# Norms folded into the stages that use them, in two token halves, with x spilled to DRAM tile by tile

## The reference

```python
# block 1
h = _modulate(x, norm_mix_w, sh1, sc1)
x = x + g1 * _merge(...)
x = x + g2 * _swiglu(_modulate(x, norm_ffn_w, sh2, sc2), w_ffn_gate, w_ffn_up, w_ffn_down)
# block 2
h = rms_norm(x) * (1 + sc1) + sh1
u = h @ w_in                      # feeds four mixers: ssd, attention, mlstm, hyena
x = x + g1 * (concatenate([y_ssd, y_na, y_ml, y_hy]) @ w_out)
h = rms_norm(x) * (1 + sc2) + sh2
x = x + g2 * ((silu(h @ ffn_w_gate) * (h @ ffn_w_up)) @ ffn_w_down)
return rms_norm(x, final_norm_g)
```

## Time and profile before

| | |
|---|---|
| median of three runs | 4113.08 us |
| the profiled execution, its own time | 4116.84 us |
| its span, first to last instruction | 4114.8 us |
| PE busy | 3665.1 us, 89% of the span |
| DVE busy | 1719.8 us, 42% |
| ACT busy | 1010.2 us, 25% |
| POOL busy | 106.5 us, 3% |
| mean granted TensorE clock | 0.921 |
| DMA | 279.54 MB, mean 68 GB/s |

### The profile page before, as it was taken

The page is one execution under the profiler, slowest core; times in us unless marked ns, Lnnn a source line. Parts: engine busy times, 40 slices in busy tenths (PEclk is TensorE's granted clock), DMA queues, the critical chain, the costliest instruction groups (busy, mean ns, idle before and its releaser), DMA issues. The chain is left out here.

```text
span 4114.8 us, 40002 instructions
## 1 busy us (share of the span) xinstructions
PE 3665.1 (89%) x15842; PEld 2752.2 (67%) x15842; DVE 1719.8 (42%) x2951; ACT 1010.2 (25%) x1635; POOL 106.5 (3%) x180
## 2 busy tenths in 40 slices
PE   7769999988879997999999797797868779999997
PEld 4345565655668776888888576675446658888885
DVE  4334431435532315444444545335574333334334
ACT  1434422212242213111111323252110131111112
POOL 0000000000010000000000000100000000000000
PEclk8888899899689998999999898898979889999999
DMA  5300020000033212222221213314223111111110
GB/s 206 134 25 1 1 100 31 11 21 11 1 105 120 92 73 92 77 92 82 72 82 61 89 57 78 99 58 138 54 92 138 46 51 41 51 51 51 41 51 41
DMA packets 72797, 279.54 MB, mean 68 GB/s; under 512 B 10424, under 2 KB 29880, under 8 KB 54873
## 3 DMA queue, kind: packets, MB, share of 16 engines
q1 hardware_dynamic: 35080, 166.63, 11.8%
q0 software_dynamic: 20928, 102.66, 6.8%
q10 hardware_dynamic: 16656, 8.42, 1.3%
HBM read 246.11 MB, written 31.59 MB: 67 GB/s over the span
## 5 line engine op out<-in xcount | busy, mean ns | idle before, releaser
L1720 PE MATMUL banks<-input_parts,weight_parts 128*128 128x512 f32 x1408 | 549.9, 391 | 47.1 <-DVE weight_parts L1772 47.1
L1721 PE MATMUL banks<-input_parts,weight_parts 128*128 128x512 f32 x1408 | 549.6, 390 | 0.0
L1722 PE MATMUL banks<-input_parts,weight_parts 128*128 128x512 f32 x1408 | 549.5, 390 | 0.0
L1720 PEld LDWEIGHTS banks<-input_parts,weight_parts 128*128 128x128 f32 x1408 | 265.7, 189 | 103.8 <-issue 48.7
L1785 DVE TENSOR_TENSOR before_split<-before_split,banks 128x512 f32<-128x512 f32 x88 | 60.6, 688 | 594.5 <-PE banks L1722 594.5
L1794 DVE SCALAR_TENSOR_TENSOR x<-banks,parameters,x 128x512 f32<-128x512 f32 x352 | 254.8, 748 | 126.9 <-PE banks L1722 126.6
L1722 PEld LDWEIGHTS banks<-input_parts,weight_parts 128*128 128x128 f32 x1408 | 265.5, 189 | 55.3
L1721 PEld LDWEIGHTS banks<-input_parts,weight_parts 128*128 128x128 f32 x1408 | 265.5, 189 | 55.2
L1720 PE MATMUL banks<-hidden_parts,weight_parts 128*128 128x512 f32 x704 | 273.9, 389 | 0.0
L1721 PE MATMUL banks<-hidden_parts,weight_parts 128*128 128x512 f32 x704 | 273.9, 389 | 0.0
L1722 PE MATMUL banks<-hidden_parts,weight_parts 128*128 128x512 f32 x704 | 273.9, 389 | 0.0
(11 more groups left out here) (496 smaller groups left out, 5971.4 us busy)
## 6 DMA issues: line engine op xcount, KB each, us to landing
weight_ring<-in_w_gu SPq DMA_DIRECT2D x44, 1024.0 KB, 4.8
weight_ring<-in_mod_w POOLq DMA_DIRECT2D x24, 1024.0 KB, 5.3
weight_ring<-in_w_down SPq DMA_DIRECT2D x22, 1024.0 KB, 4.8
weight_ring<-in_w_merge SPq DMA_DIRECT2D x24, 512.0 KB, 3.6
weight_ring<-in_dft SPq DMA_DIRECT2D x12, 1024.0 KB, 5.0
x<-in_x_t POOLq DMA_DIRECT2D x2, 4096.0 KB, 18.0
weight_ring<-in_w_ada_rest POOLq DMA_DIRECT2D x8, 1024.0 KB, 5.4
work<-in_w_ada_rest POOLq DMA_DIRECT2D x8, 1024.0 KB, 5.3
```

Of the source, the lines that this page charges most:

```text
L1720: e.matmul(bank, w_hi, hi, start=(k == 0), stop=False)
L1721: e.matmul(bank, w_hi, lo, start=False, stop=False)
L1722: mm = e.matmul(bank, w_lo, hi, start=False, stop=(k == len(terms) - 1))
```

## The change

The squares of x are made where x is written: in `linear_split` and in the last step of `ffn`, ScalarE squares each piece after its eviction and VectorE adds the squares up over the tiles (`Squares`). `SplitNorm` takes the place of the stages norm_ffn_1, norm_ffn_2, scales_2 and norm_mix_2. It runs at the start of `ffn` and of the stage "projections": one ones-matmul per half, both Ln ahead of both Exp, then scale and parts of the first token half, the first weights, and scale and parts of the second half. TensorE starts on the first half when that is ready, and waits for the second half ahead of bank q = 2 (in `ffn`) or piece 1 (in the projections). x goes to DRAM in 8 DMAs of 512 KB, each after its tile's last eviction, on SyncE. norm_final uses the ready sums, and the output is stored in four DMAs of 1 MB from the scaled pieces. `norm` (norm_mix and norm_final) makes all Ln ahead of all Exp. In ssd_outputs all 10 tokens and in mlstm's outputs all 8 come ahead of the outputs on TensorE, and ScalarE makes the second chunk's exponentials in ssd ahead of the first tokens. A group whose slot was held by single-tile weights is split one piece later. `alternate` goes to another place and is loaded at the start of the projections.

```diff
+class Squares:
+    def __init__(self, pg):
+        m = Mem(pg.big, M_H, M_PARTS)
+        self.sums, self.buf = m(2, HALF), m(2, HALF)
+        self.x = pg.x
+        self.squared, self.added = pg.shared_sem("norm_squares", 2 * KT), pg.shared_sem("norm_added", 2 * KT - 2)
+    def square(self, e, i):
+        tile, s = divmod(i, 2)
+        if i >= 4:
+            self.added.wait(e, i - 3)
+        dst = self.sums[:, s, :] if i < 2 else self.buf[:, s, :]
+        e.activation(dst, self.x[:, tile, s * HALF:(s + 1) * HALF], ACT.Square).then_inc(self.squared.sem, 1)
+    def add(self, e, i):
+        s = i % 2
+        self.squared.wait(e, i + 1)
+        if i >= 4:
+            self.added.wait(e, i - 3)
+        e.tensor_tensor(self.sums[:, s, :], self.sums[:, s, :], self.buf[:, s, :], ALU.add).then_inc(self.added.sem, 1)
...
+class SplitNorm:
+    def __init__(self, pg, scale, shift, high, low, y, rs=None, kept=None):
+        self.pg, self.scale, self.shift, self.high, self.low, self.y, self.kept = pg, scale, shift, high, low, y, kept
+        self.squares = pg.squares
+        self.rs = pg.squares.sums if rs is None else rs
+        self.ms, self.rt = pg.shared_sem("norm_sums", 2), pg.shared_sem("norm_roots", 2)
+        self.scaled, self.rounded, self.split = (pg.shared_sem(f"norm_{n}", 2 * KT) for n in ("scaled", "high", "split"))
+    def half(self, s):
+        return slice(s * HALF, (s + 1) * HALF)
+    def sums(self, e):
+        for s in range(2):
+            e.matmul(self.pg.ps[:, s, :], self.pg.ones, self.squares.sums[:, s, :], start=True, stop=True).then_inc(self.ms.sem, 1)
+    def roots(self, e):
+        rs = self.rs
+        for s in range(2):
+            self.ms.wait(e, s + 1)
+            last = e.activation(rs[:, s, :], self.pg.ps[:, s, :], ACT.Ln, bias=self.pg.eps[:, 0:1], scale=1.0 / D)
+        self.pg.achain(e)(last)
+        for s in range(2):
+            e.activation(rs[:, s, :], rs[:, s, :], ACT.Exp, scale=-0.5).then_inc(self.rt.sem, 1)
+    def take_high(self, e, s):
+        for k in range(KT):
+            self.scaled.wait(e, KT * s + k + 1)
+            e.activation(self.high[:, k, self.half(s)], self.y[:, k, self.half(s)], ACT.Identity,
+                         bias=self.shift(k)).then_inc(self.rounded.sem, 1)
+    def take_low(self, e, s):
+        if self.kept is not None and s == 0:
+            e.wait_ge(self.kept, 16 * KT)
+        self.rt.wait(e, s + 1)
+        h = self.half(s)
+        for k in range(KT):
+            e.scalar_tensor_tensor(out=self.y[:, k, h], in0=self.pg.x[:, k, h], scalar=self.scale(k), in1=self.rs[:, s, :],
+                                   op0=ALU.mult, op1=ALU.mult).then_inc(self.scaled.sem, 1)
+        for k in range(KT):
+            self.rounded.wait(e, KT * s + k + 1)
+            e.scalar_tensor_tensor(out=self.low[:, k, h], in0=self.y[:, k, h], scalar=self.shift(k),
+                                   in1=self.high[:, k, h].bitcast(F32), op0=ALU.add, op1=ALU.subtract).then_inc(self.split.sem, 1)
...
             tiles(4, KT)
-        for g in range(1, NG):
-            weights(g)
+        weights(1)
+        for g in range(NG):
+            if g + 2 < NG:
+                weights(g + 2)
+            for q in range(fills):
+                i = fills * g + q
+                e.wait_ge(pg.ps_free, f0 + i + 1)
+                squares.square(e, i)
...
+                if fills * g + q >= 4:
+                    squares.add(e, fills * g + q - 2)
...
+        for i in range(NG * fills - 2, NG * fills):
+            squares.add(e, i)
...
-        for s, w in enumerate(spans):
+        for s, w in enumerate(spans if squares is None else []):
             for k in range(KT):
                 e.activation(dst(s)[:, k, :], src(s)[:, k, :], ACT.Square).then_inc(sq.sem, 1)
         for s, w in enumerate(spans):
             ms.wait(e, s + 1)
-            ch(e.activation(rs[:, s, 0:w], pg.ps[:, s, 0:w], ACT.Ln, bias=pg.eps[:, 0:1], scale=1.0 / D))
+            last = e.activation(rs[:, s, 0:w], pg.ps[:, s, 0:w], ACT.Ln, bias=pg.eps[:, 0:1], scale=1.0 / D)
+        ch(last)
+        for s, w in enumerate(spans):
             e.activation(rs[:, s, 0:w], rs[:, s, 0:w], ACT.Exp, scale=-0.5).then_inc(rt.sem, 1)
         if shift is not None:
             for s, w in enumerate(spans):
                 for k in range(KT):
...
+            if squares is not None:
+                e.matmul(pg.ps[:, s, :], pg.ones, squares.sums[:, s, :], start=True, stop=True).then_inc(ms.sem, 1)
+                continue
...
+        for k in range(KT if spill else 0):
+            e.wait_ge(pg.ps_free, first_fill[NS - 1] + 2 * k + 2)
+            e.dma_start(spill[0][:, k, :], x[:, k, :]).then_inc(spill[1], 16)
...
+                if n == 0 and q % 2 == 0:
+                    norm.split.wait(e, KT * (q // 2 + 1))
...
+        norm.sums(e)
...
+            elif n == NS - 1:
+                hid_split.wait(e, 2 * FT)
+                for q in range(16):
+                    e.wait_ge(pg.ps_free, first_fill[n] + q + 1)
+                    squares.square(e, q)
+        norm.roots(e)
+        norm.take_high(e, 0)
         take_high(0, 0)
+        norm.take_high(e, 1)
...
+                    if n == NS - 1 and q >= 4:
+                        squares.add(e, q - 2)
+                if n == NS - 1:
+                    squares.add(e, 14)
+                    squares.add(e, 15)
             modulate(mods(n)[1], i)
+        norm.take_low(e, 0)
         take_low(0, 0)
+        norm.take_low(e, 1)
         if mod:
             row_ready.wait(e, 1)
...
-                at = max(at, self.last[same[-1]] + (self.first[g] - self.last[same[-1]] > 1))
+                old = same[-1]
+                at = max(at, self.last[old] + (self.freed[old] is None or self.first[g] - self.last[old] > 1))
...
+            if p < 2:
+                self.norm.split.wait(e, KT * (p + 1))
...
-            yield 4
+            yield SSD_PACE
             s2_rd.wait(e, c + 1)
             for hh in range(4):
                 mm = e.matmul(pg.ps[:, 2 + c % 2, hh * 64:hh * 64 + 64], Mm[:, c % 2, hh, :], XB[:, c, hh * 64:hh * 64 + 64],
                               start=True, stop=True)
             mm.then_inc(y_rd.sem, 1)
-            yield SSD_PACE - 4
     def scalar(e):
...
-            yield SSD_PACE
+            if c:
+                yield SSD_PACE
+        yield SSD_PACE
...
-            yield 3
+            yield ML_PACE
             if c:
                 y_cp.wait(e, c)
             for hh in range(4):
...
-            yield ML_PACE - 3
...
-        self.proj.landed(e, "hy")
-        e.dma_start(self.alt, pg.d["alternate"]).then_inc(self.tables.sem, 16)
...
-        self.tables.wait(e, 48)
+        self.tables.wait(e, 32)
...
+    norm_2 = SplitNorm(pg, lambda k: pg.sc2a[:, k:k + 1], lambda k: pg.mod2[:, k:k + 1], pg.mix_high, pg.mix_low, x,
+                       Mem(pg.big, M_STAGED, M_END)(2, HALF), pg.kept)
...
+    pg.alt = pg.pp[:, 0:P + 1]
...
+        e.wait_ge(pg.stage_done, 3 * after)
+        e.dma_start(pg.alt, pg.d["alternate"]).then_inc(proj.tables.sem, 16)
...
+    def tensor(e):
+        norm_2.sums(e)
+        whole(first["tensor"])(e)
+    def scalar(e):
+        norm_2.roots(e)
+        norm_2.take_high(e, 0)
+        proj.highs(e, 0)
+        norm_2.take_high(e, 1)
+        whole(first["scalar"])(e)
+    def vector(e):
+        e.tensor_scalar(pg.sc2b, pg.mod2[:, 32:40], 1.0, None, ALU.add)
+        pg.vchain(e)(e.tensor_scalar(pg.sc2a, pg.mod2[:, 8:16], 1.0, None, ALU.add))
+        norm_2.take_low(e, 0)
+        proj.lows(e, 0)
+        norm_2.take_low(e, 1)
+        whole(first["vector"])(e)
+    pg.stage(name="projections", sync=sync, gpsimd=pool, tensor=tensor, scalar=scalar, vector=vector)
...
+    def store(e, scaled):
+        for n in range(4):
+            s, k = divmod(4 * n, KT)
+            scaled.wait(e, 4 * (n + 1))
+            at = slice(s * HALF, (s + 1) * HALF)
...
-            e.dma_start(out, result).then_inc(stored, 16)
-            e.wait_ge(stored, 16)
+            e.wait_ge(pg.stored, 64)
```

148 lines of the change are left out of this document (48 added, 100 removed).

## The result

| | before | after |
|---|---|---|
| time, median (us) | 4112.01 (4108.95 to 4113.71, 4 runs) | 4038.93 (4029.26 to 4044.17, 4 runs) |
| ratio, 95% interval | | 0.982 (0.9801 to 0.984) |
| the profiled execution: time, span (us) | 4116.84, 4114.8 | 4044.17, 4042.5 |
| mean granted clock | 0.921 | 0.920 |

The change saves 73 us. I had forecast 4032, with a range of 4018 to 4051; the forecast's own case ran from 4023 to 4041. The time is in both, 7 us above the figure. The kernel before has 4112.01 here, and not the 4113.08 given above, because a fourth run has been added to its three.

The account below looks back on a forecast made before the run. TensorE was taken as busy for 89% of the span, with time lost only where it stands still. The terms summed to -80.9 us, taking the median from 4113.08 to 4032 us, range 4018 to 4051.

Parts of the forecast that it names:

- The start of the FFNs: At ffn_1 and ffn_2, squares and second-half scaling leave TensorE's path: -18.5 us each, bounds -15 to -20.
- ffn_1 to the projections: Ahead of the projections, first matmul 22.4 us earlier, but piece 1 waits 4 to 5: -15 us, bounds -8 to -18.
- The end: At the final norm and store, scaling starts earlier and the last 1 MB store follows: -12.7 us, bounds -8 to -13.5.
- ssd: In ssd's output chunks, six uncovered stalls of 2.1 to 2.2 us replace the old stalls: -1 us, bounds -5 to +7.
- mlstm: In mlstm's output chunks, outputs cover the wait for the mix, but the spread comes late: -12 us, bounds -4 to -19.
- The late split: Behind ssd_out, ScalarE's weights wait no longer holds TensorE at the barrier for 4.72 us: -4 us, bounds -5 to 0.
- (a): Second halves of the split norms late everywhere: 3.5 us at each FFN, 5 at the projections; 4044 us, 12%.
- (b): The woven stages move their stalls and do not remove them: ssd at +7, mlstm at -4; 4048 us, 14%.
- (c): The woven stages gain all, with the clock held: mlstm -19, ssd -5; 4021 us, 9%.
- (d): One table load less at each of four norms, since one set holds Ln and Exp: -5 us, 4027 us, 4%.
- (e): The last part of x's copy to DRAM lands late and the projections' scaling waits 7 us; 4039 us, 5%.
- (f): A 2 us stall at every chunk keeps the clock low through both woven outputs: up to +140, 4172 us; 2%.

Follow-up runs that it names:

- the combined kernel: The kernel after with ssd's outputs behind 6 tokens and ahead of 4, FFNs' first weights on VectorE, early table load, Ln and Exp per half: 4009.47 us.

## Why the prediction was right, and where it was off

**The start of the FFNs (-18.5 each; measured -17.4 and -16.7).** Right in mechanism: no wait came ahead of the third bank, the second half was never late. One overlap was wrong, and with it a term: "4.7 from the barrier to the first scaling, the two ones-matmuls run beside the table load". They do not. The load is issued behind ScalarE's wait for the first sum, so it was 6.74 at ffn_2 and 5.9 at ffn_1. The run with the early load showed that the load alone is not the whole error: the second sum is late as well, and only both edits together give 4.8.

**ffn_1 to the projections (-15; -15.9).** The copy of x held nothing, piece 1 waited 5.64. The late root cost 1.8 us here too (6.51 for 4.7) and piece 1 waited a little longer than forecast; the stretch behind made that good, which lies within the spread of 3 us and is not explained further.

**The end (-12.7; -11.7).** The same late root, 1.2 of it.

**The first norm (+1.5; +1.56).** Right, and shown alone.

**ssd (-1; +1.8 by the means, -0.7 with the order alone on the kernel before, a single profile).** The six bare stalls came exactly as described. Neither figure can be told from nothing in a stretch that the clock spreads over 4 us. I took the clock to be a wash between old and new stalls; that it is worth 5 us once the stalls go was not in my text.

**mlstm (-12; -15.6).** Two terms were too small: the stalls shrank by 12.2 and not 9.4, and the clock gave 6.3 and not 2.6 (with the order alone). I had set the chunk at its length without any low clock and so made the spread late too often.

**The late split (-4; -5.5) and `alternate` (-0.7; -1.3).** The 4.7 us at the barrier go as described, but TensorE's restart, to which I credited the gain, is not what counts: the stretch ends when the attention's values land, and GpSimd, held by the same wait of ScalarE, issues them 3.8 us earlier. I had not seen that path; the size came out right since both hang on one wait. Taking the late split back gives 3.6 of the 5.5; of the rest, 0.9 is that the values took 15.7 us from issue to landing in the mean of the five kernels before, and 14.8 in the eight after. That another table would set the time in place of `alternate` was the step that kept 12 us out of the forecast.

**The total.** The changed stretches gave -80.8 for -80.9. That is partly luck: the starts of the FFNs and the end missed 3.8, ssd 2.8; mlstm, the split, `alternate` and the projections gave 6.6 more. The 7 us between 4032 and the median are not in them, and since a time without a profile can't be split into stretches, where they lie is not shown. The unedited code is uneven enough for them: the kernel before had a median of 4112 in the four runs beside the kernel after and of 4118 in the nine beside the combined kernel, and from 4118 the same sum gives 4037. The forecast took unedited code at what one profile had; two in fourteen profiles had 11 us more in the front, and the start ran over 11 us from the shortest to the longest. The range had no term for this; it held because it was wide for other reasons.

**The rivals.** (a) late second halves: no wait in the FFNs. (b) and (c): mlstm and ssd came between them. (d) no load went: the kernel after has one ahead of Ln and one ahead of Exp (3280.01 and 3282.58). The Trainium skill, "ScalarE: Activation LUTs", section "Table sets: the hidden batching unit", has Ln and Exp in one set; in the combined kernel there are loads of 1.28 us at 3257.39, 3259.33 and 3261.33, one at every change between the two, so the trace disagrees again. (e) did not come: the scaling at the projections waited for no copy. (f) the clock held low through both outputs: it was 0.93 over ssd's and 0.92 over mlstm's in the kernel after; it did not happen.

## What to carry to other kernels

An operation that only prepares an engine (a table load, a first weight split) starts behind the wait that stands ahead of it in the queue, also when it doesn't need what is waited for; look at what the engine does while it waits, put the preparation there, and then look for the second thing that was due at the same time. What a barrier costs is not only the wait of the busiest engine behind it: look at what every queue that it holds issues next, here GpSimd's load. When work is woven, a consumer placed directly behind its producer is bare however much filler the turn has: split the filler (6 and 4 in place of 10 and 0), and count the clock with the stall. Compare single stretches over all profiles of kernels that share them; the total of one execution can hide or invent 10 us.

## What the runs showed of the hardware

- The same code had two lengths in one stretch, 1383 to 1388 and 1397 us, with a granted clock of 0.83 or 0.72 over the same 461 matmuls. The same kernel had both. Ahead of it the same 224 matmuls kept TensorE busy for 63.7 to 73.3 us.
- Two sums by four ones-matmul records took 1.99 us at one place and 3.66 at the other, after the same idle time of 2.94, at a granted clock of 1.00 and 0.53.
- With six stalls of 2.12 us TensorE was busy for 109.8 to 110.6 us over the same 520 matmuls in six profiles of kernels after (113.1 in a seventh, and 109.2 on the kernel before); with one of 1.54 and of 1.45 for 104.8 and 103.5. That the stalls cause the difference is argued from these kernels; no run varied the stall's length alone.
- The last of three loads of the attention's values landed 14.0 to 17.6 us after its issue, over fourteen profiles.
- VectorE's rounding copy of 128x2048 took 1.23 us, ScalarE's 1.89, and the subtraction of the same size 2.29.
